# The launch of a two-layer hybrid backbone: slots 0 and 1 contracted one feature block at a time, with ScalarE's and VectorE's order rearranged

## The reference, cut to what matters

```
for l in range(2):
    mod_l = (silu(c) @ w_ada[l] + b_ada[l])        # 9 vectors of 1024: shift, scale, gate, three times
    mod_c = (silu(c_ctx) @ w_ada[l] + b_ada[l])    # the same for the context tokens
    xl = ffn(xl, mod_l, 0); xc = ffn(xc, mod_c, 0) # x + 0.5*gate*rmsnorm(swiglu(pre(x)))
    ... mixer (Fourier groups and bidirectional mLSTM), then a second ffn
pre(x) = rmsnorm(x, nw) * (1 + scale) + shift
swiglu(h) = (silu(h @ w_g) * (h @ w_u)) @ w_out
```

## Time and profile before

| | us |
|---|---|
| median of three runs | 2501.41 |
| lowest and highest | 2501.26 and 2507.79 |
| the profiled execution | 2496.65 |
| its span, first to last instruction | 2494.9 |

### The profile page before, as it was taken

How to read it: one execution, slowest core, us unless ns; L and a number is a source line. 1 busy time by engine, 2 the same in 40 slices (tenths; PEclk the granted TensorE clock), 3 DMA queues, 4 the chain that set the end, 5 groups by cost and what they waited for, 6 DMA issues and landing times.

```text
span 2494.9 us, 35459 instructions
## 1 busy us (share of the span) xinstructions
PE 2427.3 (97%) x13552; PEld 2209.6 (89%) x13552; DVE 1874.5 (75%) x2362; ACT 1126.9 (45%) x1627; POOL 611.9 (25%) x429
## 2 busy tenths in 40 slices
PE   7999999999999999999999999999999998999998
PEld 4999998888977899999888999999888777899987
DVE  5799997776577779888766799876656677888733
ACT  5343443444453744443353544444444555555522
POOL 0344440000500034444000144550000500266400
PEclk9999999999999999999999999999999999999999
DMA  6333336542111243323643433337443213422331
GB/s 258 110 126 131 145 128 254 185 160 82 52 48 47 107 161 133 119 109 135 245 160 135 169 112 126 143 142 256 166 144 99 80 37 106 148 101 101 118 118 67
DMA packets 100368, 328.33 MB, mean 132 GB/s; under 512 B 7809, under 2 KB 38049, under 8 KB 86945
## 3 DMA queue, kind: packets, MB, share of 16 engines
q1 hardware_dynamic: 83040, 316.33, 35.1%
q10 hardware_dynamic: 17218, 10.55, 1.4%
HBM read 318.28 MB, written 8.57 MB: 131 GB/s over the span
## 4 chain that ended last, share of the span: by engine, by line
PE 77%; DVE 14%; issue 4%; ACT 3%; DMA 2%; POOL 0%; DVEq 0%; SPq 0%; ACTq 0%; POOLq 0%
PE ps L2206 29%; PE ps L2166 27%; PE ps L2154 8%; PE ps L928 5%; DVE junk L1764 3%; DVE w_all L2014 2%; DVE w_all L1744 1%; DMA acc<-w_ada_t 1%; PE ps L2248 1%; DVE arena L669 1%; PE ps L997 1%; PE ps L1068 1%; PE ps L1044 1%; PE ps L952 1%; PE ps L1055 1%
## 5 line engine op out<-in xcount | busy, mean ns | idle before, releaser
L2206 PE MATMUL ps<-w_all,hj_all 128*128 128x512 f32 x2856 | 654.3, 390 | 5.2 <-DVE arena L828 2.5
L2206 PEld LDWEIGHTS ps<-w_all,hj_all 128*128 128x128 f32 x2856 | 534.1, 188 | 117.8 <-DVE arena L828 2.9
L2166 PE MATMUL ps<-xn_hi,w_all 128*128 128x384 f32 (+1 forms) x2592 | 614.0, 319 | 9.8 <-DVE gate_row L2067 8.4
L1744 DVE TENSOR_TENSOR w_all<-raw,w_all 128x2048 fp32r<-128x2048 f32 x138 | 321.9, 2332 | 267.5 <-ACT w_all L1387 267.4
L2166 PEld LDWEIGHTS ps<-xn_hi,w_all 128*128 128x128 f32 x2592 | 450.3, 190 | 17.6 <-DVE gate_row L2067 16.2
L2166 PE MATMUL ps<-xn_lo,w_all 128*128 128x384 f32 (+1 forms) x1296 | 411.5, 318 | 0.0
L1387 ACT ACTIVATE w_all<-raw 128x2048 fp32r<-128x2048 f32 x139 | 262.6, 1889 | 241.0 <-PE ps L2206 201.2
L2014 DVE TENSOR_TENSOR w_all<-raw,w_all 128x1024 fp32r<-128x1024 f32 (+1 forms) x216 | 324.1, 1502 | 36.6 <-ACT w_all L1609 36.3
L1764 DVE SCALAR_TENSOR_TENSOR junk<-acc,silu_row 128x1024 bf16<-128x1024 f32 x224 | 334.8, 1495 | 14.7 <-issue 6.4
L1609 ACT ACTIVATE w_all<-raw 128x1024 fp32r<-128x1024 f32 (+1 forms) x216 | 197.9, 918 | 259.0 <-PE ps L2166 246.9
L2154 PE MATMUL ps<-xn_hi,w_all 128*128 128x384 f32 (+1 forms) x1024 | 246.2, 324 | 9.8 <-DVE xn_lo L1822 7.6
(11 more groups left out here) (236 smaller groups left out, 3212.9 us busy)
## 6 DMA issues: line engine op xcount, KB each, us to landing
raw<-w_ff_in SPq DMA_DIRECT2D x104, 1024.0 KB, 4.8
raw<-w_ff_out SPq DMA_DIRECT2D x77, 1024.0 KB, 5.0
acc<-w_ada_t SPq DMA_DIRECT2D x128, 512.0 KB, 3.3
raw<-w_out SPq DMA_DIRECT2D x16, 1024.0 KB, 4.8
raw<-w_in SPq DMA_DIRECT2D x12, 1024.0 KB, 5.8
x<-x_in SPq DMA_DIRECT2D x12, 512.0 KB, 10.8
gate_row<-gate_out_rows ACTq DMA_DIRECT2D x12, 512.0 KB, 6.2
x_out<-x SPq DMA_DIRECT2D x12, 512.0 KB, 9.1
```

The source lines that it names most:

```text
L1744: nc.vector.tensor_tensor(w_lo[par][:, 0:width], raw[par][:, 0:width], w_hi[par][:, 0:width].bitcast(F32), ALU.subtract).then_inc(S["w_lo" ...
L2166: ins = mm(ps[:, bank_, 0:xx[0].shape[-1]], w[:, c], x_[:, k, :], start=start and k == 0 and a == 0, stop=k == 3 and a == 2, skip_group_ch ...
L2206: ins = mm(ps[:, 2 * i + hf, :], xx[:, i * P:(i + 1) * P], w[:, c, hf * 512:(hf + 1) * 512], start=first and c == 0 and a == 0, stop=last ...
```

## The change

Scale and shift are made block by block. SP brings the shift as eight units of 512 KB (`w_ada0[k]`, 128 outputs each; units 0 to 5 land in pieces of 512 B, 6 and 7 in pieces of 4 KB), and the scale as eight units of 512 KB, mixed with x and the two slots. PE contracts each shift unit with silu(c) stationary (8 matmuls of 128 columns). DVE forms one block of the latent scale at a time. The three tiles are turned before they are modulated and copied to `xT_first` in SBUF; for each block k ACT modulates and rounds [128 x 384], DVE takes the rest (`first_low`), and PE multiplies that block's part of slots 0 and 1 (`first_part`: six matmuls each). The context's scale and everything for tiles 3 to 5 come behind block 7, in `first_lead`, which replaces `lead` for this sublayer only.

```diff
+        def scale_unit(k):
+            if k == KC - 1:
+                return acc[:].rearrange("p a n -> p (a n)")
+            return at(A_H + (4 * GW, A_DUMMY - A_H + D, HG, HG + D, HG + 2 * D, HG + 3 * D, HG + KC * HB + 3 * D)[k], D)
+        def shift_unit(k):
+            if k < 2 * GT:
+                block = at(k // GT * KC * TOK, KC * TOK).rearrange("p (k t) -> p k t", k=KC)
+                return block[:, :, GW + k % GT * P:GW + (k % GT + 1) * P]
+            return gate_row[:, k - 2 * GT, :].rearrange("p (k n) -> p k n", k=KC)
...
-            return (6, 2, 4)[i]
+            return (0, 4, 0)[i]
...
+            def shift(k):
+                sp.dma_start(shift_unit(k), w_ada0[k]).then_inc(S["shift_raw"][k], 16)
+            def scale(k):
+                sp.dma_start(scale_unit(k), w_ada_t[0, KC + k]).then_inc(S["scale_raw"][k], 16)
...
             sp.dma_start(cvec[:], cvec_in).then_inc(S["c_in"], 16)
-            first_half(0)
+            shift(0)
+            sp.dma_start(x[:, 0, :], x_in[0]).then_inc(S["x_first"][0], 16)
+            shift(1)
+            for t in range(1, GT):
+                sp.dma_start(x[:, t, :], x_in[t]).then_inc(S["x_first"][t], 16)
             for dst, src in ((b_col[:], b_col_in), (nw_col[:], nw_col_in)):
                 sp.dma_start(dst, src).then_inc(S["early_consts"], 16)
-            first_units(2, (0, 1))
-            first_half(1)
-            first_units(2, (2,))
-            load_x(range(GT), "x_in")
-            first_units(2, (3,))
-            first_units(3, range(2))
-            last_columns()
+            shift(2)
+            shift(3)
+            scale(0)
             load(0, 0, w_ff_in[0, 0, 0])
+            scale(1)
+            scale(2)
+            shift(4)
+            load(1, 1, w_ff_in[0, 0, 1])
+            for k in range(5, KC):
+                shift(k)
+            sp.dma_start(silu_row[:, 1, :], c_row_in[:, 1, :].to_broadcast([P, D])).then_inc(S["c_late"], 16)
+            for k in range(3, KC):
+                scale(k)
             load_x(range(GT, NT), "x_late")
...
-            pool.wait_ge(S["mod_made"], 1)
...
+            def turned_copy(t):
+                act.wait_ge(S["xT"], t + 1)
+                b = first_bank(t)
+                nc.scalar.activation(xT_first[:, :, t * P:(t + 1) * P], ps[:, b:b + 2, :].rearrange("p b (c w) -> p (b c) w", w=P),
+                                     ACT.Copy).then_inc(S["xT_sb"], 1)
+            def first_stat(t):
+                act.wait_ge(S["x_first"][t], 16)
+                prenorm_stat(t, t, t)
             act.wait_ge(S["row_spread"], 1)
+            nc.scalar.activation(silu_row[:, 0, :], psum_tile(1), ACT.Copy).then_inc(S["silu_row"], 1)
             act.wait_ge(S["pool_consts"], 2)
+            first_stat(0)
+            first_stat(1)
+            prenorm_scale(0, 0, 0)
+            first_stat(2)
+            prenorm_scale(1, 1, 1)
+            prenorm_scale(2, 2, 2)
+            turned_copy(0)
             split_w(0, 0)
+            turned_copy(1)
+            turned_copy(2)
+            act.wait_ge(S["xT_sb"], GT)
             for k in range(KC):
+                act.wait_ge(S["first_mod"], k + 1)
+                part = xT_first[:, k, :]
+                nc.scalar.activation(part, part, ACT.Identity, scale=scale_col[:, k, 0:1], bias=m_shift[:, k, 0:1]).then_inc(S["first_act"], 1)
+                act.wait_ge(S["first_act"], k + 1)
+                nc.scalar.activation(xn_hi[:, k, 0:GW], part, ACT.Copy).then_inc(S["first_hi"], 1)
+                if k == 1:
+                    split_w(1, 1)
+                if k == 2:
+                    act.wait_ge(S["c_late"], 16)
+                    nc.scalar.activation(silu_row[:, 1, :], silu_row[:, 1, :], ACT.Silu).then_inc(S["silu_row"], 1)
...
+            def late_turned(sub, i):
+                act.wait_ge(S["xT"], GT + i + 1)
+                act.wait_ge(S["mod_made"], 1 if i == 0 else 2)
...
+                for k in range(KC):
+                    part = ps[:, b + k // 4, (k % 4) * P:(k % 4 + 1) * P]
+                    s = 0 if i == 0 else 1
+                    ins = nc.scalar.activation(part, part, ACT.Identity, scale=m_scale[:, k, s:s + 1], bias=m_shift[:, k, s:s + 1])
+                ins.then_inc(S["mod_act"], 1)
+                act.wait_ge(S["mod_act"], 1 if i == 0 else 2)
+                act.sem_inc(S["modded"], 1)
+            def first_lead(sub):
+                tile = lambda i: (GT + i, GT + i, turn_bank((0, 0), i))
+                act.wait_ge(S["x_late"], 16 * (NT - GT))
+                prenorm_stat(GT, GT, GT)
+                prenorm_scale(GT, GT, GT)
+                gate_silu(sub, 0, 0, 0, 0, (0,))
+                split_w(2, 0)
+                gate_silu(sub, 1, 1, 1, 1, (0,))
+                prenorm_stat(GT + 1, GT + 1, GT + 1)
+                prenorm_stat(GT + 2, GT + 2, GT + 2)
+                prenorm_scale(GT + 1, GT + 1, GT + 1)
+                prenorm_scale(GT + 2, GT + 2, GT + 2)
+                split_w(3, 1)
+                late_turned(sub, 0)
+                prenorm_split(*tile(0))
+                prenorm_split(*tile(1))
+                gate_silu(sub, 2, 2, 2, 0, (0,))
+                split_w(4, 0)
+                late_turned(sub, 2)
+                prenorm_split(*tile(2))
+                gate_silu(sub, 3, 3, 3, 1, (0,))
...
+            def scale_part(k, s):
+                dve.wait_ge(S["scale_raw"][k], 16)
+                if parts:
+                    dve.wait_ge(S["ada0_used"], len(parts))
...
+                nc.vector.scalar_tensor_tensor(out=junk[:], in0=scale_unit(k), scalar=1.0, in1=silu_row[:, s, :], op0=ALU.mult,
+                                               op1=ALU.mult, accum_out=scale_sum[:, k, s:s + 1]).then_inc(S["ada0_used"], 1)
+            def first_low(k):
+                dve.wait_ge(S["first_hi"], k + 1)
+                nc.vector.tensor_tensor(xn_lo[:, k, 0:GW], xT_first[:, k, :], xn_hi[:, k, 0:GW].bitcast(F32), ALU.subtract).then_inc(S["first_lo"], 1)
+            def shift_rows(i):
+                dve.wait_ge(S["shift_mm"], 4 * i + 4)
+                nc.vector.tensor_copy(shift_sb[:, i, :], ps[0:2, 6 + i, :]).then_inc(S["shift_sb"], 1)
+            def shift_cols(i):
+                dve.wait_ge(S["shift_cols"], i + 1)
...
+            dve.wait_ge(S["early_consts"], 16 * 2)
...
+            dve.wait_ge(S["scale_one"], 1)
+            shift_rows(0)
+            for k in range(KC):
+                scale_part(k, 0)
+                dve.wait_ge(S["ada0_used"], len(parts))
+                own.link(nc.vector.scalar_tensor_tensor(out=scale_col[:, k, 0:1], in0=scale_sum[:, k, 0:1], scalar=scale_bias[:, k:k + 1],
+                                                        in1=nw_col[:, 0, 0, k:k + 1], op0=ALU.add, op1=ALU.mult))
+                shift_cols(k // 4)
+                dve.sem_inc(S["first_mod"], 1)
+                if k and k != 3:
+                    first_low(k - 1)
+                if k == 2:
+                    dve.wait_ge(S["w_lo"], 1 + START)
+                    split_w(1, 1)
+                    first_low(2)
+                if k == 3:
+                    shift_rows(1)
+                    dve.wait_ge(S["silu_row"], 2)
+                    scale_part(0, 1)
+            first_low(KC - 1)
+            nc.vector.tensor_copy(m_scale[:, :, 0:1], scale_col[:, :, 0:1]).then_inc(S["mod_made"], 1)
+            dve.wait_ge(S["first_lo"], KC)
+            for name in ("modded", "xn_hi", "xn_done"):
+                dve.sem_inc(S[name], GT)
...
+            def first_lead(sub):
+                bank = [turn_bank((0, 0), i) for i in range(GT)]
+                scale_part(1, 1)
+                prenorm_rs(GT, GT)
+                for k in range(2, 4):
+                    scale_part(k, 1)
+                gate_mul(sub, 0, 0, 0, (0,))
+                split_w(2, 0)
+                gate_mul(sub, 1, 1, 1, (0,))
+                for k in range(4, 6):
+                    scale_part(k, 1)
+                prenorm_rs(GT + 1, GT + 1)
+                prenorm_rs(GT + 2, GT + 2)
+                make_consts()
+                for k in range(6, KC):
+                    scale_part(k, 1)
+                dve.wait_ge(S["ada0_used"], 2 * KC)
+                own.link(nc.vector.tensor_tensor(scale_col[:, :, 1], scale_sum[:, :, 1], scale_bias, ALU.add))
+                nc.vector.tensor_tensor(m_scale[:, :, 1], scale_col[:, :, 1], nw_col[:, 0, 0, :], ALU.mult).then_inc(S["mod_made"], 1)
+                dve.wait_ge(S["mod_made"], 2)
+                dve.sem_inc(S["fin_read"], 4)
+                split_w(3, 1)
+                prenorm_lo(GT, GT, bank[0])
+                prenorm_mod(GT + 1, GT + 1, bank[1])
+                prenorm_lo(GT + 1, GT + 1, bank[1])
+                gate_mul(sub, 2, 2, 0, (0,))
+                split_w(4, 0)
+                prenorm_lo(GT + 2, GT + 2, bank[2])
                 gate_mul(sub, 3, 3, 1, (0,))
...
+            def shift(k):
```

(62 more changed lines are left out.)

183 lines of the change are left out of this document (57 added, 126 removed).

## The result

The forecast was wrong. Over 20 runs of each kernel the medians are 2508.68 us (2500.90 to 2515.28) for the changed kernel and 2502.47 us (2498.14 to 2508.53) for the one before; the ratio is 1.0024, its 95% interval 1.0016 to 1.0032. The change loses 4 to 8 us where 2.5 of gain were forecast, and 2508.68 lies outside the range. The profiled executions took 2503.57 and 2496.65 us, the spans 2501.8 and 2494.9.

What follows compares the result with a forecast made beforehand. Loads bound the launch to 33.6 us, DVE to 45.0, ScalarE (free at 46.3) for 33.7 more: slot 4 at 80.0, not 82.5. The 2.5 us gain, off the median 2501.4, gives 2498.9 us; range 2493 to 2505.

Steps and rivals of the forecast that it cites:

- The step that failed: From slot 4 to the fast products: DVE's and POOL's sums begin near 80 us, covered by four slots of 8.3 us.
- Slot 4 at 80.0: End of the launch: block 7 done at 46.3 us plus 33.7 puts slot 4 at 80.0, against 82.5 before.
- stretch 3: `first_lead`, block 7 to slot 4, bound by ScalarE: instructions of 27.6 us plus waits, together 33.7 us.
- some 0.5: Blocks 3 to 7: DVE's wait for PE's last shift unit, some 0.5 us of that stretch's 11.4.
- All else in the launch lies beside these loads: Up to scale block 3: PE's 14.4 us of shift, ScalarE's norm and POOL's subtraction fit within the loads' time.
- The rest moves with slot 4: From slot 4 on, same instructions, four slots of 8.3 us; the rest of the 2500 us moves with that moment.
- The loads: Up to scale block 3: 512 B pieces take 1.8 us a unit, six cost 3.0 us more; scale 3 lands at 33.6.
- Rival B: Loads: 512 B pieces cost no extra, scale 3 lands at 30.6 us; 5.5 us earlier, 2495.9 us. Chance 0.12.
- C: Slower loads: 512 B units above 1.8 us; at 2.6 a unit 2503.7 us, at 4.4 2514.5. Chance 0.13.
- Slots 0 and 1 done near 51.5: Behind block 7: PE has slots 0 and 1 done at about 51.5 us, 13 us ahead of 64.95.
- Rival A: Stretch 3: lead hides behind PE, slots 2 and 3 without waits, slot 4 13 us early; 2488.4 us. Chance 0.06.
- Rival D: Half clock behind PE's wait of about 3 us before slot 4 loses 1.7; gain 0.8, 2500.6 us. Chance 0.27.

Runs made afterwards that it cites:

- e6: Changed kernel, but GpSimd's two sums of the first sublayer wait only for slot 3's low part and tile 3's turn, not all six tiles; ratio to before 1.0006.
- e4: Kernel before, but GpSimd's and VectorE's sums for the fast products held until PE has done slot 3; ratio to before 1.0027.
- e1: Changed kernel, but slot 0's low part made on VectorE instead of GpSimd; one run, 2504.99 us.
- e5: Changed kernel, but PE contracts shift units 5 to 7 ahead of slot 0's parts for blocks 1 and 2; one run, 2505.90 us.
- e7: Changed kernel with the edits of e1, e5 and e6 together; ratio to before 0.9997.
- e8: e7 with stretch 3 reordered: early squares, square roots in a row, context's row early, tile 4 turned before slot 2; ratio to before 0.9968.
- e10: e9 with the square roots of tiles 4 and 5 back behind the silus of slots 0 and 1; one run, 2498.65 us.
- e2: Changed kernel, but VectorE splits slot 5 ahead of its two sums in the first sublayer; ratio to before 1.0020.
- e3: Changed kernel, but GpSimd's sums of the first sublayer wait for slot 5's low part; ratio to before 1.0016.
- e9: e8, but PE turns tile 4 behind slot 2 again, not ahead of it; one run, 2496.38 us.

## Why the prediction was wrong

**The step that failed.** "DVE's sums for the fast products, and POOL's, wait for all tiles and so begin near 80, not near 72; they have four slots of 8.3 us to be done in, which I count as enough cover." In the trace of before only GpSimd's sums begin near 72; VectorE's begin at 83.5, and at 86.2 after the change. So what the change did is to lay the two side by side. I saw that the sums would lie beside slots 4 to 7 and counted the slots, not the work. Between slot 4 and the fast products VectorE now has 10.6 us of sums, 6.9 of splits and 5.9 of other work with both inputs in SBUF, and GpSimd 7.0 us of sums and 5.2 of smaller ones. As these go one after the other, that is 35.6 us beside 33.3 of PE's (each at its undisturbed length); before the change it was 28.6. It cost 5.5 us (e6 against the changed kernel); put into the kernel before by itself it costs 6.1 (e4, "between"). The next sentence, "Without it the fast products would begin late by what is missing", was right, but it had neither a price nor a chance, and none of the rivals contained it. The row that tells it was in the trace of before: a split of 4.56 us beside GpSimd's sums, where 2.29 is usual. It is not the only one: at 149.96 us, for instance, a sum of 128x8 takes 1.12 us beside GpSimd, where its twins take 0.17. I had not looked at durations that stand out where nobody waits. The Trainium skill has the rule (SBUF — State Buffer, section SBUF: two separate sides): VectorE and GpSimd share a pair of ports that is held for a whole instruction, and a VectorE instruction with two SBUF inputs takes part in it. The trace agrees: VectorE's 0.22 us instruction ended at 26.20, 0.02 behind GpSimd's that had begun 0.02 us before it, and with one input in PSUM 1.23 us stayed 1.23.

**Slot 4 at 80.0.** It came at 85.9. Of the 5.9, 0.8 belong to stretch 3 (34.5 against 33.7, so that sum was right) and 5.1 to block 7, at 51.4 instead of 46.3. Its terms: the scale's unit 3 at 34.6 instead of 33.6, 1.0; the wait for PE's last shift unit 4.0 instead of "some 0.5", 3.5; small ones the rest. The wait had two causes that overlap. "All else in the launch lies beside these loads" was wrong twice. GpSimd's subtraction, which I had moved to 21 us without asking whom it meets, held VectorE's small instruction (e1: 2.8 us). And PE did not "work as they land" on its eight units of 1.8 us, since slot 0's parts stood ahead of unit 7 and PE ran there partly at the half clock (0.54 from 22 to 33 us; e5: 3.3 us). Together they are worth 4.4 (e7), less than their sum.

**The rest moves with slot 4.** Right in form where the sums are covered (33.4 in e6, e8 and e10, 33.3 before), wrong in the changed kernel (38.9).

**The loads.** The scale's unit 3 landed at 34.6: the price of the 512 B pieces, 1.8 us a unit, held within 1.0 us for six units. Rival B (30.6) is out: in the changed kernel, e1, e2, e3, e5 and e7 VectorE's wait for this unit ended between 34.1 and 35.3. With it, here, goes the Trainium skill's 512 B at line rate (DMA: Bandwidth & Descriptors, Specifications). That the pieces' size is the cause is argued from their price; no run loads the same bytes in larger pieces. Of C there was only this 1.0 us. The loss came by a mechanism that had no rival, and my range ended where C's moderate case did, at 2505.

**Slots 0 and 1 done near 51.5.** It was 59.9; from 43 to 50 us PE ran at 0.52 of the clock, after it had waited 2.8 us. It cost next to nothing: slot 2's weights were split only at 61.4, and though ScalarE waited 0.8 us for slot 1, in e7, where it did not, the stretch from block 7 to slot 4 took 34.5 us as well.

**Rival A**, the lead hidden, is out. PE waited 0.8 us before slot 2, 2.8 before tile 5's transpose and 1.1 before slot 4, where I had put 3 each time; it was later itself. **Rival D**, the clock: the stretch that counts was real, and cost 1.7 us as priced, but it stood behind the wait before slot 5, not before slot 4. In e7, where the wait before slot 4 is 2.7 us, it is found just where D had put it.

## What to carry to other kernels

When a change moves work of one engine in time, look at every engine that will then run beside it, and ask of each pair on VectorE and GpSimd whether VectorE's instruction has an operand in PSUM. If it has none, count their times as added up: so it was with two inputs in SBUF, and with the one conversion of a single input. Cover is counted as work against time on each engine, not as a number of slots. In the trace of before, search for instructions that took longer than their twins, also where nobody waits: such a row shows a conflict that the change may bring onto the path. And before work is shortened, ask what each consumer really reads: GpSimd's sums waited for six tiles and read three.

## What the runs showed of the hardware that I had not expected

A VectorE instruction on 128x1 elements took 4.50 us beside GpSimd's subtraction of 4.50, and 0.22 with GpSimd idle. Sums of 1.77 us each took 4.9, and GpSimd's second one 5.0 instead of 3.5: the two engines took turns, an instruction each. With one operand in PSUM nothing was slowed in e6. A conversion with a single input, in SBUF, was (e8: 3.39 us instead of 0.22). GpSimd needs 4.50 us for the subtraction that VectorE does in 2.29, so in e1 the work was moved to the engine that does it twice as fast. A table load costs ScalarE's list 1.3 us: after the change the root starts at 53.78, 1.30 behind the start of its load. The 1.38 us of drain that the Trainium skill adds (ScalarE: Activation LUTs, What ACT_TABLE_LOAD costs) is seen at no switch of the launches, neither ahead of the load nor behind it. PE waits of 2.1 (e2), 2.5 (e3), 2.7 (e7), 2.8 (e9), 4.0 and 4.3 us before a slot were followed by a stretch at about half the clock that cost 1.3 to 1.7 us. Waits of 1.1 and 1.9 were not, nor were one of 2.4 (e5, before slot 5) and one of 2.7 (e7, before tile 5's transpose), behind which the clock stayed at 1.00. So the length of a wait alone does not tell it. Not settled: in the profiled executions, the lag over the kernel before shrinks by 1 to 2 us between 300 and 1460 us in the changed kernel, e2 and e6, and grows in e4; the reason was not looked for.
